# Who multiplies the probabilities of the second block's attentions: VectorE or GpSimd

## The reference, cut to what matters

```python
# layer 0, eight MLA heads: latent queries see context and latent keys, context queries see context keys
sc = q_lat . c_kv + q_rope . k_rope
p  = softmax(sc * scale);  o = p . c_kv
# layer 0, eight neighbourhood heads: a bias (rel_bias, or NEG_INF outside the window) on the latent keys
p  = softmax(concat([s_ctx, s_lat + col_bias]));  o = p . v
# layer 1, sixteen sliding-window heads, only latent queries; a sink joins the denominator
p  = softmax(concat([sink, s_ctx, where(band_ok, s_lat, NEG_INF)]));  o = p[1:] . v
```

## Time and profile before

| | |
|---|---|
| time, median of 3 runs | 2715.67 us (2712.34 to 2717.53) |
| the profiled execution | 2718.1 us, its span 2716.3 us |
| busy share of the span: PE, PEld, DVE, ACT, POOL | 89%, 54%, 26%, 19%, 0% |
| attention of layer 0 | from about 1666 to 1762 us of the span |
| attention of layer 1 | from about 2366 to 2427 us of the span |
| granted TensorE clock in both | 1.00 |

### The profile page before, as it was taken

One profiled execution on the slowest core, in us unless ns is written; L12 is line 12 of the kernel. 1 busy time (PEld: TensorE's weight loads), 2 busy tenths in 40 slices (PEclk: granted clock), 3 DMA queues, 4 the chain that ended last, 5 costly groups with the idle time before them and its releaser, 6 DMA issues.

```text
span 2716.3 us, 37487 instructions
## 1 busy us (share of the span) xinstructions
PE 2409.6 (89%) x15842; PEld 1466.3 (54%) x15842; DVE 697.6 (26%) x1553; ACT 517.9 (19%) x1018; POOL 0.2 (0%) x4
## 2 busy tenths in 40 slices
PE   6998749997995888888886889989999998899997
PEld 3553418886884344444443335734444443688886
DVE  2058593333113111111111105620000001251001
ACT  3111522221002111111111214611000001151001
POOL 0000000000000000000000000000000000000000
PEclk8999769998996999999998999999999999999999
DMA  8263083321330989888987120011222122203431
GB/s 326 72 245 155 6 359 114 112 102 64 139 109 22 376 364 371 370 368 363 371 371 301 47 108 1 2 62 62 77 77 78 62 77 81 78 27 130 150 130 62
DMA packets 59589, 434.06 MB, mean 160 GB/s; under 512 B 6592, under 2 KB 6848, under 8 KB 7360
## 3 DMA queue, kind: packets, MB, share of 16 engines
q1 hardware_dynamic: 57744, 420.50, 39.6%
q10 hardware_dynamic: 1712, 11.58, 1.1%
HBM read 431.01 MB, written 1.05 MB: 159 GB/s over the span
## 4 chain that ended last, share of the span: by engine, by line
PE 80%; DVE 8%; DMA 7%; issue 2%; ACT 2%; SPq 0%; DVEq 0%; ACTq 0%
PE bank L513 78%; DMA ring<-in_w 6%; PE bank L624 1%; ACT normed L1177 1%; DMA arena<-in_xin 1%; DVE small L1474 0%; DVE arena L1867 0%; DVE arena L1625 0%; SPq L1970 0%; PE bank L559 0%; DVE arena L1860 0%; DVE arena L1507 0%; DVE arena L1506 0%; DVE arena L1605 0%; DVE rs_t L1447 0%
## 5 line engine op out<-in xcount | busy, mean ns | idle before, releaser
L513 PE MATMUL bank<-normed,ring 128*128 128x512 f32 (+1 forms) x2688 | 877.5, 487 | 37.3 <-issue 27.5
L513 PEld LDWEIGHTS bank<-normed,ring 128*128 128x128 f32 x2688 | 514.3, 192 | 395.1 <-issue 340.2
L513 PE MATMUL bank<-arena 64*64 64x64 f32 (+6 forms) x6896 | 441.1, 251 | 53.4 <-DVE arena L1867 14.6
L513 PE MATMUL bank<-ring,arena 128*64 128x512 f32 (+1 forms) x1824 | 397.3, 611 | 49.6 <-DMA ring<-in_w 25.1
L513 PEld LDWEIGHTS bank<-arena 64*64 64x64 f32 (+4 forms) x6896 | 361.5, 146 | 140.5 <-issue 110.0
L513 PE MATMUL bank<-arena,ring 128*128 128x256 f32 (+1 forms) x1024 | 298.5, 453 | 2.8 <-DVE arena L1923 1.3
L513 PEld LDWEIGHTS bank<-ring,arena 128*64 128x64 f32 (+1 forms) x1824 | 140.5, 136 | 279.0 <-issue 249.3
L513 PEld LDWEIGHTS bank<-arena,ring 128*128 128x128 f32 x1024 | 194.2, 190 | 105.5 <-issue 84.4
L1923 DVE TENSOR_TENSOR arena<-arena,bank 128x512 f32<-128x512 f32 (+1 forms) x44 | 24.4, 554 | 431.5 <-PE bank L513 431.5
L513 PE MATMUL bank<-ring,normed 128*32 128x512 f32 (+2 forms) x576 | 115.9, 597 | 8.3 <-DMA ring<-in_w 8.3
L513 PE MATMUL bank<-arena,con 128*128 128x256 f32 (+5 forms) x304 | 92.4, 437 | 24.2 <-DVE small L1802 11.1
(11 more groups left out here) (280 smaller groups left out, 1349.7 us busy)
## 6 DMA issues: line engine op xcount, KB each, us to landing
ring<-in_w SPq DMA_DIRECT2D x401, 1024.0 KB, 6.9
arena<-in_xin ACTq DMA_DIRECT2D x1, 2048.0 KB, 8.3
arena<-in_nab ACTq DMA_DIRECT2D x1, 2048.0 KB, 11.2
con<-in_con ACTq DMA_DIRECT2D x1, 1472.5 KB, 11.4
sw<-in_sw ACTq DMA_DIRECT2D x1, 1280.0 KB, 10.5
sw<-in_sw ACTq DMA_DIRECT2D x1, 1168.0 KB, 10.4
arena<-in_xin ACTq DMA_DIRECT2D x1, 1024.0 KB, 13.0
out<-arena ACTq DMA_DIRECT2D x1, 1024.0 KB, 4.0
```

The costliest lines, as they stand in the source:

```text
L513: return nc.tensor.matmul(o, l, r, start=start, stop=stop, **kw)
```

## The change

VectorE stops after the reciprocal in the attentions named "even" (layer 0) and "swa" (layer 1) and raises a new semaphore, `inverse_even` or `inverse_swa`. GpSimd gets a function that waits for it, pair by pair, and does the two multiplications, which raise `prob_` as before. The combined pairs of the first block keep their code; only the line of the reciprocal moves into their branch.

```diff
-                        v.does(V.reciprocal(inv, it["den"]))
                         if it["comb"]:
+                            v.does(V.reciprocal(inv, it["den"]))
                             v.does(tt(inv[:, 1:2], inv[:, 1:2], neglam, MUL))
...
                         else:
-                            for x in range(2):
-                                ts(p[x][:, 0:nk], p[x][:, 0:nk], inv[:, x:x + 1], None, MUL)\
-                                    .then_inc(S("prob_" + name), 1)
+                            V.reciprocal(inv, it["den"]).then_inc(S("inverse_" + name), 1)
...
+        @block.gpsimd
+        def _(pool):
+
+            def normalise(name, pairs):
+
+                for u, it in enumerate(pairs):
+                    nk, p, inv = it["nk"], it["p"], it["inv"]
+                    pool.wait_ge(S("inverse_" + name), u + 1)
+                    for x in range(2):
+                        nc.gpsimd.tensor_scalar(p[x][:, 0:nk], p[x][:, 0:nk], inv[:, x:x + 1], None, ALU.mult)\
+                            .then_inc(S("prob_" + name), 1)
+
+            normalise("even", even_pairs())
+            normalise("swa", swa_pairs())
```

## The result

The changed kernel takes 2754.97 us (median of 4 runs, 2751.72 to 2756.62), against 2716.36 for the kernel before on the same chip: 1.0141 of it, 95% interval 1.0127 to 1.0154, or 38.6 us more. Forecast was 2722, at most 2740. The sign held, and so did the prediction's law for a stall; the size was six times too small, and the course was that of rival C: GpSimd falls behind, and layer 1 stalls for every second pair.

What follows compares the result with a forecast made beforehand. TensorE was taken to bound the kernel, busy 82.98 of 83.00 and 40.00 of 40.00 us in the attentions. Stalls of 0.4 + 1.5 + 3.2 + 1.04 + 0.2 + 0.2 = 6.5 us gave 2722.2 against median 2715.67; range 2714 to 2740.

Steps and rivals of the forecast that it cites:

- the prediction's law for a stall: In each pair TensorE stalls 0.12 + 2T us less the room from reciprocal's end to second head's transposes.
- rival C: Both attentions: GpSimd is slow (T = 1.3, short 0.7) and falls behind; 22 us more, 2740; chance 0.23.
- T: Time of one 128x512 multiplication on GpSimd, chosen as 0.90 us between 0.48 and 3.35; a short one 0.50.
- first pair of layer 0: Short pair at the start of layer 0's attention: room 0.72 us, stall 0.40 us.
- three MLA groups: Layer 0, first long pairs of three groups of MLA heads: stalls 0.52, 0.52 and 0.43 us, together 1.5.
- four groups of R = 1.12: Layer 0, four pairs with 1.12 us from reciprocal's end to second head's transposes: stalls 4 x 0.80 = 3.2 us.
- end of layer 0: Last two pairs of layer 0: four multiplications move the last transposes from 1758.89 to 1759.93, 1.04 us.
- layer 1, start: First pair's second transposes come 0.86 us later; TensorE had 0.66 to wait, so 0.2 us is lost.
- layer 1, middle: Middle of layer 1's attention: 1.92 us is less than the room of 2.03, so nothing is lost.
- layer 1, end: Last but one pair's fourth transposed quarter ends at 2423.19, where TensorE went on at 2422.99: 0.2 us.
- B: Both attentions: GpSimd is quick (T = 0.55, short 0.35) and nothing is lost; +0.2 us, 2718.3; chance 0.29.
- The exclusive lock: VectorE instructions with two SBUF inputs and GpSimd's SBUF reads exclude each other; changes nothing in the forecast, only rival C meets it.

Runs made afterwards that it cites:

- kernel with the other form of the instruction: The whole change, with GpSimd multiplying two tensors (reciprocal read again for each column) instead of tensor by scalar: 1.0032 of the kernel before, +8.6 us.
- the early order with GpSimd: The whole change with each pair's reciprocal ahead of the next pair's maxima: 1.0048 of the kernel before; with GpSimd's two-tensor form 1.0057.
- the last kernel with one head: Against the kernel before: GpSimd's two-tensor form for layer 0's pairs 2 to 30, reciprocal early there; in layer 1, old order, for head 1 only: 1.0002.
- layer 1 alone: The change in layer 1's attention only, layer 0's multiplications left on VectorE: 1.0050 of the kernel before, +14 us.
- the early order on VectorE: The kernel before with each pair's reciprocal and multiplications ahead of the next pair's maxima, none on GpSimd: 1.0084, +23 us.

## Why the prediction was wrong

**The step that failed is one number: T, the length of a 128x512 multiplication on GpSimd**, put at 0.90 (0.50 short) and measured at 1.57 (0.93). The text bounded it by 0.48 and 3.35 and chose near ScalarE's 0.63; rival C stopped at 1.3. Everything that hung on T moved with it:

| term | forecast | its formula with T = 1.57 | measured |
|---|---|---|---|
| first pair of layer 0 | 0.4 | 1.3 | 1.3 |
| three MLA groups | 1.5 | 3 x 2.5 = 7.4 | 7.3 |
| four groups of R = 1.12 | 3.2 | 4 x 3.04 = 12.2 | 13.5 |
| end of layer 0 | 1.04 | 3.7 | 3.7 |
| layer 1, start | 0.2 | 1.5 | 3.1 |
| layer 1, middle | 0 | 5.5 x 1.23 = 6.8 | 7.1 |
| layer 1, end | 0.2 | 2.6 | 2.6 |
| sum | 6.5 | 35.5 | 38.6 |

The third column uses the prediction's rule for a group in which GpSimd falls behind (four multiplications after the first reciprocal) and its rule for every second pair of layer 1; both were written for rival C and both held. The measured column is read from reciprocal to reciprocal in the two traces, and at the end of each attention to the last transpose. In rival C itself the start of layer 1 was reckoned too high: at T = 1.3 the first transposes come 1.66 late, and with the 0.66 of waiting taken off, as in the forecast, 1.0 is left and not 1.6.

**What bounds the kernel** was right: nothing was won by 34 us less on VectorE, and GpSimd's 26 us on the short pairs cost nothing.

**The hand-overs** were put at 0.06 to GpSimd and 0.06 from it, and are 0.08 and 0.04 (the chain above), together the same 0.12. **First use** cost nothing that shows.

**What the formula leaves, 3.1 us**, is mostly a term that the prediction did not have. TensorE's granted clock in the attentions was 1.00 throughout before. In the changed kernel, after waits of about 1 us for GpSimd, it falls to half, for 10.2 us in all. Such a wait does not bring the fall each time: the first two whole neighbourhood groups have the same waits (1.02 and 0.89) and keep 1.00. Busy times by stretch (PE, PEld, DVE, ACT, POOL, clock, DMA):

```profile
1767.00:1769.50 2.50, 2.50 (x15) 1.52 (x15) 0.50 (x2) 0.60 (x1) 2.01 (x2) 0.50 0.00 0
...
2400.00:2404.00 4.00, 3.45 (x15) 2.33 (x16) 0.00 (x0) 1.60 (x4) 3.58 (x3) 0.62 0.00 0
```

0.50 of 2.4 GHz is the lower level, 1.2 GHz. In the chain of the changed kernel the same kind of work is longer there:

```profile
1721.91 2.21 PE bank L513 x12
1724.12 1.52 PE bank L624 x8
```

Against 1.22 and 1.02 at full clock. The two groups with the fall take 15.38 us, the others 14.69 or 14.70: 0.7 each, 1.4 together. At the start of layer 1 the scores of one pair take 2.95 instead of 1.76, 1.2 more. That makes 2.6 of the 3.1 us. It is read from the traces. The kernel with the other form of the instruction, in which the clock did not fall, met the formula in layer 0 within 0.1 us, which fits; but no experiment took the clock away by itself, so this part is argued and not shown.

**The rivals.** C was the right one (slow, falls behind, layer 1 stalls for every second pair), 22 us at T = 1.3. B's rule from the Trainium skill, GPSIMD Engine Reference, section 4.1 Engine selection (one input at about line rate, two inputs about twice as slow as on VectorE), agrees for two tensors, 1262 ns against VectorE's 692, and not for the instruction of this change: one tensor and a scalar took 1564 ns against VectorE's 483, where a copy took 612. The exclusive lock was weighed and set aside with the right result for this change, in which VectorE's instructions all kept their length; it was the experiments with the two-tensor form that it decided.

**Where the reasoning should have gone otherwise.** The chances were built as if T lay symmetrically around 0.9. With one end at 0.48 and the other at 3.35, the upper side was worth far more. The price was low as well: the prediction put 1.8 us on each 0.10 in T. Its own terms give 2.3 at T = 0.90, and 5.0 once the second long pair waits for the first to leave GpSimd and the middle of layer 1 stalls (4 x 0.4 + 3 x 0.4 + 0.4 + 0.1 in layer 0, 0.2 + 5.5 x 0.2 + 0.4 in layer 1). The range should have reached to T = 1.6 or more, by these terms about 2753.

## What to carry to other kernels

Before work is moved to another engine, compare the room between its input and its consumer with the length there, and with the queue of the same work behind it: 26 us of GpSimd cost nothing on the short pairs, while two multiplications of 1.57 us against 1.12 of room, with two more behind them, cost 3 us in each neighbourhood group. An operation that no trace shows has to be measured first, in every form that gives the same result; here the form alone was worth 1.57 against 1.04. And to relieve an engine that has time to spare wins nothing while another one is full.

## What the runs showed of the hardware that I had not expected

- GpSimd multiplies 512 columns by a scalar from SBUF in 1564 ns, by a constant in 1488, two tensors in 1262, and by one column read again for every element in 1039. Copy 612, memset 524.
- Two engines in one place are not one case. GpSimd's multiplication by a scalar leaves VectorE's two-column operation at 0.16 us and lengthens itself from 1.57 to 1.86 beside VectorE's multiplication; in an unbroken stream of these it took 1.61, and VectorE's went from 0.49 to 0.79 and 0.84. GpSimd's two-tensor form keeps its 1.04 and makes VectorE wait: 0.16 becomes 0.92, 0.48 becomes 1.36.
- The granted clock fell only where TensorE had waited, and not each time that it had. In layer 0 it fell in the two kernels with the whole change there (6.8 us each). In layer 1 it fell for 3.4 us in the changed kernel, in the early order with GpSimd (all pairs, either form) and in the last kernel with one head, for 6.8 with layer 1 alone, and for 10.2 in the early order on VectorE. In the kernel before and in the other five of the attention experiments it stayed at 1.00.
